# Two transformer blocks on one core: moving the rows of the first matmul operand inside its buffer

## The chip, the cores and the metric

The kernel runs on one core of one Trainium2 chip. The metric is the device time of one execution in microseconds; before the change it is 2463.79 us, the median of 3 runs (2463.78 to 2463.86).

## The reference, cut to what matters

Two blocks follow each other on 256 tokens of width 2048, everything in float32. The first has 16 meta tokens ahead of the 256.

```python
# first block: D = 2048, D_FF = 5632
z = rmsnorm(h) @ w_in                 # q, k, v, gate_b, gate_c, hc, forget logits
y = concat(forgetting_attention(q, k, v, log_f), gate_b * short_conv(gate_c * hc))
h = h + rmsnorm_by_group(y) @ w_out
h = h + (silu(n @ w_gate) * (n @ w_up)) @ w_down        # n = rmsnorm(h)
x = rmsnorm(h)[:, 16:]
# second block: D_FF_2 = 8192
q, k, v, u, gate_attn, gate_pool = split(x @ w_in_2)
merged = sigmoid(gate_attn) * (attention(q, k, v) @ w_ba) + sigmoid(gate_pool) * (pool(u) @ w_bp)
x = layer_norm(a * x + merged @ w_out_2)
x = layer_norm(a * x + square(relu(x @ w_ff1)) @ w_ff2)
```

Nearly all of the work is the products with the weights. Everything between them is small.

## The kernel before, in words

**A product in three parts.** Every float32 matrix is split into a high and a low part, each of a type (float32r) that TensorE takes at one column a cycle. A product A x W is computed as high A x high W, low A x high W and high A x low W. Here W is the stationary operand (128 x 128) and A, stored with features on the partitions and tokens along the free axis, is the moving one. An output tile of 128 features x 256 tokens is summed in a PSUM bank over all K tiles (pieces of 128 input features), and there are 16 of those for a width of 2048.

**Steps.** Weights stream from memory in units of 128 x 1024 float32 (512 KB) that hold two K tiles for a block of four output tiles. ScalarE copies a unit to `w_hi` (L842), VectorE subtracts to get `w_lo` (L1235), and four units are kept split. A step of TensorE's program is one unit for one output tile, in the code of `product_step`. For the 256 tokens it takes four matmuls, called a group below:

1. L606: `w_hi` of the even K tile times high and low rows at once, 512 columns (bank halves 0 and 1)
2. L607: `w_lo` of the even K tile times the high row, 256 columns
3. L609: `w_lo` of the odd K tile times its high row, 256 columns
4. L610: `w_hi` of the odd K tile times its high and low rows, 512 columns

Then the same two K tiles follow for the next of the four output tiles. Stages with 272 or 258 columns do not fit two rows in a bank and take three matmuls for each K tile (L613 to L615) instead.

**Two operands.** Stages alternate between operand buffers `a_op` and `b_op`, so that one can be filled while the other is read. `a_op` is used in two ways. Early, for the stages k, f, q, v and conv, K tile kt is at `a_op[:, kt, i, 0:272]`, with i 0 for high and 1 for low. Later the same memory is seen through `a_late`, which has 8 rows of 1088 words, one for each pair of K tiles, and is used for gu, k2, q2, v2, u, gate, out2 and ff2. `part` gives one row of 256 columns in it, and `parts` gives both rows of a K tile as one access pattern of 2 x 256. ScalarE writes the high rows (L961, L1028, L1033, L1098) and VectorE the low rows (L1456, L1611, L1687) through `part`.

**Places.** The word place is used from here on for the byte offset of a row within its tensor modulo 256. In `a_late` and `b_op` the rows of a pair of K tiles start at words 48, 306, 564 and 822 in the order high, low, high, low, which is at places 192, 200, 208 and 216. The 1088 words of a pair are 17 x 256 bytes, so that every pair has the same places. `h`, `a_op`, `b_op`, `raw`, `w_hi` and `w_lo` are allocated one after another with sizes that are multiples of 256 bytes, so places in them compare with each other. A 128-column slice of the weights starts at a multiple of 512 bytes, which is place 0. In the early use with 256 columns (stage q and the gate_b tiles of conv), the even K tile has its high row at place 64 and its low row at 128, and the odd K tile has them at 192 and 0.

**What sets the order.** The order of every engine is written out by a plan (`make_plan`) and semaphores, and no address enters it. TensorE's program goes on with the next unit when VectorE has split it (`lo_split`).

Of the kernel before, what the change touches and what calls it, by code (L numbers as in the profile page):

```python
# [19 lines left out]
TOK = META + SEQ  # L20
# [161 lines left out]
def two_blocks(nc, w, tokens, params, consts, mask1, mask2, positions, out):  # L182
# [5 lines left out]
    with ExitStack() as ctx:  # L188
        def sb(name, shape, dt=F32):
            return ctx.enter_context(nc.sbuf_tensor(name, shape, dt))  # L190
# [3 lines left out]


        ROW, PLACE = SEQ + 2, 48
        ROWS2 = 32 + HEADS
        h = sb("h", [P, KT, TOK])
        a_op = sb("a_op", [P, KT, 2, TOK], F32R)
        a_late = a_op[:, :, :, :].rearrange("p k i t -> p (k i t)").rearrange("p (m c) -> p m c", m=KT // 2)  # L200
        b_op = sb("b_op", [P, KT // 2, 4 * TOK], F32R)
# [21 lines left out]

        last_slot = b_op[0:ROWS2, KT // 2 - 1, PLACE + 2 * ROW:PLACE + 4 * ROW]
        cneg, pick = last_slot[:, 0:TOK], last_slot[:, TOK:TOK + HEADS]
# [9 lines left out]
        out_bank = [ctx.enter_context(nc.psum_tensor(f"out_bank{i}", [P, 512], F32)) for i in range(OUT_BANKS)]  # L235
        side_bank = [ctx.enter_context(nc.psum_tensor(f"side_bank{i}", [P, 512], F32)) for i in range(2)]

        def part(op, kt, i, n=SEQ):

            at = PLACE + ROW * (2 * (kt % 2) + i)  # L240
            return op[:, kt // 2, at:at + n]

        def parts(op, kt, n=SEQ):
            at = PLACE + ROW * 2 * (kt % 2)
            return op[:, kt // 2, at:at + 2 * ROW].rearrange("p (i t) -> p i t", i=2)[:, :, 0:n]

        def affine_column(i, x):
            rows = b_op[:, :, PLACE:PLACE + 4 * ROW].rearrange("p m (o i t) -> p m o i t", o=2, i=2)
# [137 lines left out]
        def tiles_at(step, part, *stages):  # L386

            for t in finish.get(step - max(0, part - 1), ()):
                if t.stage in stages and t.stage != "pool":
                    yield t  # L390
# [107 lines left out]
        def tensor_program(eng):  # L498
            t_ = Lane(eng)

            def take_side(kind, key, sem_free, value):

                i = len(side_release)
                if i >= 2:
                    t_.wait_ge(*side_release[i - 2])
                side_release.append((sem_free, value))
                side_of[kind, key] = side_bank[i % 2]
                return side_bank[i % 2]
# [28 lines left out]
            def moving(blk, cols, kt):  # L537

                if blk.operand == "a" and blk.stage not in ("k", "f", "q", "v", "conv"):
                    return part(a_late, kt, 0), part(a_late, kt, 1), parts(a_late, kt)  # L540
                if blk.operand == "a":
                    lo, hi = {"all": (0, TOK), "pair": (META, TOK), "conv": (META - 2, TOK)}[cols]
                    return a_op[:, kt, 0, lo:hi], a_op[:, kt, 1, lo:hi], a_op[:, kt, :, lo:hi]
                n = ROW if cols == "affine" else SEQ
                return part(b_op, kt, 0, n), part(b_op, kt, 1, n), parts(b_op, kt, n)
# [113 lines left out]
            def first_mixer(step):  # L659
# [17 lines left out]
                if (hd := head_at(step, CONV0)) is not None:  # L677
                    bank = take_side("scores", hd, masked, 2 * hd + 2)
                    sel = pick[:, hd:hd + 1].to_broadcast([ROWS2, P])
                    t_.wait_ge(q_scaled, hd + 1)  # L680
# [543 lines left out]
        def vector_program(eng):  # L1224
# [74 lines left out]
            def first_mixer(step):  # L1299
# [6 lines left out]
                if step == FORGET:  # L1306
# [11 lines left out]
                    v_.e.tensor_scalar(z, z, bf, None, ALU.add).then_inc(forget_step)  # L1318
                    v_.e.tensor_scalar(cneg, row[0:ROWS2, :], 0.0, None, ALU.mult).then_inc(rows_zeroed)
                if step == FORGET + 15:  # L1320
# [10 lines left out]
                    v_.wait_ge(forget_step, 10)  # L1331
                    v_.e.scalar_tensor_tensor(cneg[32:ROWS2, :], csum, -1.0, cneg[H8, :].bitcast(F32), ALU.mult,
                                              ALU.subtract).then_inc(forget_step)
                    v_.wait_ge(consts_landed, 16)
                    v_.e.tensor_tensor(pick, ident[0:ROWS2, H8], ident[0:ROWS2, 32:ROWS2], ALU.add).then_inc(pick_ready)
                for tile in tiles_at(step, 1, "q"):
# [642 lines left out]
        block = ctx.enter_context(nc.Block())  # L1979
# [117 lines left out]
```

## Time and profile before

| | before |
|---|---|
| median of 3 runs | 2463.79 us |
| the profiled execution | 2463.61 us, its span 2461.8 us |
| granted TensorE clock, mean | 0.997 |
| PE busy | 2433.2 us (99%), 14730 matmuls |
| weight loads (PEld) busy | 2168.8 us (88%) |
| VectorE, ScalarE, GpSimd busy | 66%, 49%, 9% |
| DMA engines | 58% of their time in the weight queue, 182 GB/s from memory |

PE is TensorE's matmul side and PEld its weight-load side, which runs beside it. A matmul's end is modelled, so the duration of one is longer than its share of the engine: the next one starts before it. How often matmuls start tells what they cost.

### The profile page before, as it was taken

What the parts mean: (1) busy time and instruction counts of PE and PEld (TensorE: products, weight loads), DVE (VectorE), ACT (ScalarE), POOL (GpSimd) and SP (SyncE); (2) the same over time, 40 slices, a digit from 0 to 9 for tenths busy, and PEclk for the clock granted to TensorE, in tenths of its full rate; (3) what the DMA queues carried; (4) which work ended last, traced back from release to release, by engine and by line L of the source; (5) the groups of instructions that cost most, each with busy time, mean ns of one, the idle gap of its engine ahead of it and who ended that gap; (6) DMA issues with size and microseconds to landing.
All of it is one profiled execution on the core that took longest, in us unless ns stands there. A gap on an engine that the chain in (4) does not pass through costs nothing.

```text
span 2461.8 us, 36358 instructions
## 1 busy us (share of the span) xinstructions
PE 2433.2 (99%) x14730; PEld 2168.8 (88%) x14730; DVE 1623.4 (66%) x2474; ACT 1199.9 (49%) x1729; POOL 213.8 (9%) x231
## 2 busy tenths in 40 slices
PE   8999999999999999999999999999999999999996
PEld 8898998888888888888888888888998888888886
DVE  5646676766666665667677756678885665565667
ACT  6444545544444443545555654544554443443544
POOL 0001111000000000002221102033200000000022
PEclk9999999999999999999999999999999999999998
DMA  7554456665666566665555456665566666666663
GB/s 248 180 158 128 131 166 196 189 190 181 197 190 191 184 196 190 189 187 194 192 186 171 161 188 190 184 193 182 163 194 196 189 189 188 188 195 189 183 194 103
DMA packets 125752, 449.60 MB, mean 183 GB/s; under 512 B 13840, under 2 KB 16400, under 8 KB 125584
## 3 DMA queue, kind: packets, MB, share of 16 engines
q1 hardware_dynamic: 125296, 446.91, 58.2%
q8 instruction: 116, 1.90, 0.3%
q14 instruction: 52, 0.43, 0.0%
q10 hardware_dynamic: 288, 0.36, 0.0%
HBM read 445.12 MB, written 2.10 MB: 182 GB/s over the span
## 4 chain that ended last, share of the span: by engine, by line
PE 95%; DVE 3%; ACT 1%; issue 0%; DMA 0%; POOL 0%; ACTq 0%; POOLq 0%; DVEq 0%
PE out_bank L606 27%; PE out_bank L610 27%; PE out_bank L607 14%; PE out_bank L609 14%; PE out_bank L613 3%; PE out_bank L614 3%; PE out_bank L615 3%; DVE w_lo L1235 1%; ACT w_hi L842 0%; PE side_bank L725 0%; PE side_bank L716 0%; DVE h L1618 0%; DVE b_op L1680 0%; PE side_bank L740 0%; PE side_bank L686 0%
## 5 line engine op out<-in xcount | busy, mean ns | idle before, releaser
L1235 DVE TENSOR_TENSOR w_lo<-raw,w_hi 128x1024 fp32r<-128x1024 f32 x839 | 1040.4, 1243 | 594.8 <-ACT w_hi L842 590.7
L842 ACT CAST w_hi<-raw 128x1024 fp32r<-128x1024 f32 x840 | 877.9, 1049 | 958.0 <-PE out_bank L610 875.8
L606 PE MATMUL out_bank<-a_op,w_hi 128*128 128x512 f32 x1984 | 784.6, 395 | 1.2 <-DVE w_lo L1235 0.7
L610 PE MATMUL out_bank<-a_op,w_hi 128*128 128x512 f32 x1984 | 776.7, 391 | 0.0
L607 PE MATMUL out_bank<-a_op,w_lo 128*128 128x256 f32 x1984 | 558.9, 282 | 0.0
L609 PE MATMUL out_bank<-a_op,w_lo 128*128 128x256 f32 x1984 | 552.1, 278 | 0.0
L609 PEld LDWEIGHTS out_bank<-a_op,w_lo 128*128 128x128 f32 x1984 | 380.1, 192 | 84.4
L607 PEld LDWEIGHTS out_bank<-a_op,w_lo 128*128 128x128 f32 x1984 | 372.9, 188 | 76.9
L606 PE MATMUL out_bank<-b_op,w_hi 128*128 128x512 f32 x992 | 389.8, 393 | 0.0
L610 PE MATMUL out_bank<-b_op,w_hi 128*128 128x512 f32 x992 | 388.0, 391 | 0.0
L606 PEld LDWEIGHTS out_bank<-a_op,w_hi 128*128 128x128 f32 x1984 | 373.1, 188 | 3.3 <-DVE w_lo L1235 1.7
L610 PEld LDWEIGHTS out_bank<-a_op,w_hi 128*128 128x128 f32 x1984 | 373.0, 188 | 0.0
L607 PE MATMUL out_bank<-b_op,w_lo 128*128 128x256 f32 x992 | 279.7, 282 | 0.0
L609 PE MATMUL out_bank<-b_op,w_lo 128*128 128x256 f32 x992 | 275.8, 278 | 0.0
L609 PEld LDWEIGHTS out_bank<-b_op,w_lo 128*128 128x128 f32 x992 | 190.4, 192 | 42.0
L607 PEld LDWEIGHTS out_bank<-b_op,w_lo 128*128 128x128 f32 x992 | 186.3, 188 | 39.9
L606 PEld LDWEIGHTS out_bank<-b_op,w_hi 128*128 128x128 f32 x992 | 186.5, 188 | 0.0
L610 PEld LDWEIGHTS out_bank<-b_op,w_hi 128*128 128x128 f32 x992 | 186.5, 188 | 0.0
L1252 DVE TENSOR_TENSOR work<-work,out_bank 128x256 f32<-128x256 f32 x248 | 102.5, 416 | 118.2 <-ACT work L861 117.5
L613 PE MATMUL out_bank<-a_op,w_hi 128*128 128x258 f32 (+1 forms) x504 | 147.5, 293 | 0.0
L614 PE MATMUL out_bank<-a_op,w_hi 128*128 128x258 f32 (+1 forms) x504 | 144.1, 286 | 0.0
L615 PE MATMUL out_bank<-a_op,w_lo 128*128 128x258 f32 (+1 forms) x504 | 143.7, 285 | 0.0
(288 smaller groups left out, 1998.7 us busy)
## 6 DMA issues: line engine op xcount, KB each, us to landing
raw<-in_w_ff SPq DMA_DIRECT2D x256, 512.0 KB, 4.2
raw<-in_w_in SPq DMA_DIRECT2D x223, 512.0 KB, 3.8
raw<-in_w_gu SPq DMA_DIRECT2D x176, 512.0 KB, 4.2
raw<-in_w_down SPq DMA_DIRECT2D x88, 512.0 KB, 4.3
raw<-in_w_out SPq DMA_DIRECT2D x64, 512.0 KB, 4.1
raw<-in_w_ba SPq DMA_DIRECT2D x16, 512.0 KB, 4.3
raw<-in_w_bp SPq DMA_DIRECT2D x16, 512.0 KB, 4.2
out<-h SPq DMA_DIRECT2D x8, 256.0 KB, 2.1
```

What stands on the lines that cost most here:

```text
L606: t_.e.matmul(bank[:, :], wh, a_both, start=start, stop=False, skip_group_check=True)
L607: mm = t_.e.matmul(bank[:, 0:SEQ], wl, a_hi, start=False, stop=stop, skip_group_check=True)
L609: t_.e.matmul(bank[:, 0:SEQ], wl, a_hi, start=False, stop=False, skip_group_check=True)
L610: mm = t_.e.matmul(bank[:, :], wh, a_both, start=False, stop=stop, skip_group_check=True)
L613: t_.e.matmul(to, wh, a_hi, start=start, stop=False, skip_group_check=True)
L614: t_.e.matmul(to, wh, a_lo, start=False, stop=False, skip_group_check=True)
L615: mm = t_.e.matmul(to, wl, a_hi, start=False, stop=stop, skip_group_check=True)
L842: a.e.copy(w_hi[:, m % SPLIT, :], raw[:, u % RAW, :]).then_inc(hi_split)
L1235: v_.e.tensor_tensor(w_lo[:, m % SPLIT, :], raw[:, u % RAW, :], w_hi[:, m % SPLIT, :].bitcast(F32), ALU.subtract).then_inc(lo_split)
L1252: v_.e.tensor_tensor(y, y, bank_of(tile)[:, 0:SEQ], ALU.add).then_inc(bank_free)
```

## The change

Only the offsets of the rows in `a_late` change. `b_op` keeps its own, and the early use of `a_op` is not touched. The table `A_ROWS` has an entry for each four K tiles, and in it the high and low offsets in words of the even and of the odd K tile:

| K tiles | order in memory | places before: high, low; high, low | places now |
|---|---|---|---|
| 0 to 3 | high, high, low, low | 192, 200; 208, 216 | 192, 200; 192, 200 |
| 4 to 7 | high, high, low, low | 192, 200; 208, 216 | 208, 216; 208, 216 |
| 8 to 11 | high, high, low, low | 192, 200; 208, 216 | 64, 72; 64, 72 |
| 12 to 15 | high, low, high, low | 192, 200; 208, 216 | 184, 192; 200, 208 |

From a high row to its low row it is 514 words in the first three, and 258 words before and in the last. Modulo 1024 bytes both are 8 bytes. No instruction is added, removed or moved on any engine; the matmuls, the writes of the rows and all waits stay as they are, with other addresses.

```diff
+        A_ROWS = (((48, 562), (304, 818)), ((52, 566), (308, 822)), ((16, 530), (272, 786)), ((46, 304), (562, 820)))
...
+        def rows_at(op, kt):
+
+            block = 4 * TOK * (kt // 2)
+            if op is b_op:
+                return block + PLACE + ROW * 2 * (kt % 2), block + PLACE + ROW * (2 * (kt % 2) + 1)
+            hi, lo = A_ROWS[kt // 4][kt % 2]
+            return block + hi, block + lo
+
         def part(op, kt, i, n=SEQ):
 
-            at = PLACE + ROW * (2 * (kt % 2) + i)
-            return op[:, kt // 2, at:at + n]
+            at = rows_at(op, kt)[i]
+            return op[:, :, :].rearrange("p m c -> p (m c)")[:, at:at + n]
 
         def parts(op, kt, n=SEQ):
-            at = PLACE + ROW * 2 * (kt % 2)
-            return op[:, kt // 2, at:at + 2 * ROW].rearrange("p (i t) -> p i t", i=2)[:, :, 0:n]
+            hi, lo = rows_at(op, kt)
+            flat = op[:, :, :].rearrange("p m c -> p (m c)")
+            return flat[:, hi:hi + 2 * (lo - hi)].rearrange("p (i t) -> p i t", i=2)[:, :, 0:n]
```

## Rows read from the trace of the kernel before

**Rows 1.** The page: busy time, and the granted clock in 40 slices

```profile
PE 2433.2 (99%) x14730; PEld 2168.8 (88%) x14730; DVE 1623.4 (66%) x2474; ACT 1199.9 (49%) x1729; POOL 213.8 (9%) x231
...
PEclk9999999999999999999999999999999999999998
```

**Rows 2.** The page: chain of work that ended last, by engine

```profile
PE 95%; DVE 3%; ACT 1%; issue 0%; DMA 0%; POOL 0%; ACTq 0%; POOLq 0%; DVEq 0%
```

**Rows 3.** Waits of PE: who for whom, us in total, times, longest

```profile
PE out_bank L568 <- DVE a_op L1240: 6.9, 1, 6.9
PE side_bank L805 <- POOL acc L1961: 0.8, 1, 0.8
PE out_bank L606 <- DVE w_lo L1235: 0.7, 1, 0.7
```

**Rows 4.** Groups of instructions, whole span: busy us, mean ns, idle before

```profile
L1235 DVE TENSOR_TENSOR w_lo<-raw,w_hi 128x1024 fp32r<-128x1024 f32 x839 | 1040.4, 1243 | 594.8 <-ACT w_hi L842 590.7
L842 ACT CAST w_hi<-raw 128x1024 fp32r<-128x1024 f32 x840 | 877.9, 1049 | 958.0 <-PE out_bank L610 875.8 <-PE out_bank L615 77.7 <-DMA raw<-in_w_in 4.1
L606 PE MATMUL out_bank<-a_op,w_hi 128*128 128x512 f32 x1984 | 784.6, 395 | 1.2 <-DVE w_lo L1235 0.7 <-DVE h L1262 0.3
```

**Rows 5.** Timeline of PE in stage ff2: start us, duration us

```profile
2000.22 0.39 PE L606 MATMUL out_bank<-a_op,w_hi 128*128 128x512 f32 x1
2000.45 0.28 PE L607 MATMUL out_bank<-a_op,w_lo 128*128 128x256 f32 x1
2000.57 0.28 PE L609 MATMUL out_bank<-a_op,w_lo 128*128 128x256 f32 x1
2000.68 0.39 PE L610 MATMUL out_bank<-a_op,w_hi 128*128 128x512 f32 x1
...
2084.11 0.39 PE L606 MATMUL out_bank<-a_op,w_hi 128*128 128x512 f32 x1
```

**Rows 6.** Groups of PE and PEld, 1997 to 2085 us (stage ff2, `a_late`)

```profile
L606 PE MATMUL out_bank<-a_op,w_hi 128*128 128x512 f32 x128 | 50.2, 392 | 0.0
L610 PE MATMUL out_bank<-a_op,w_hi 128*128 128x512 f32 x127 | 49.7, 391 | 0.0
L607 PE MATMUL out_bank<-a_op,w_lo 128*128 128x256 f32 x127 | 35.8, 282 | 0.0
L609 PE MATMUL out_bank<-a_op,w_lo 128*128 128x256 f32 x127 | 35.3, 278 | 0.0
...
L609 PEld LDWEIGHTS out_bank<-a_op,w_lo 128*128 128x128 f32 x127 | 24.4, 192 | 5.4
L610 PEld LDWEIGHTS out_bank<-a_op,w_hi 128*128 128x128 f32 x127 | 23.9, 188 | 0.0
```

**Rows 7.** Groups of PE, 95 to 105 us (stage q, early places)

```profile
L610 PE MATMUL out_bank<-a_op,w_hi 128*128 128x512 f32 x15 | 6.0, 397 | 0.0
L606 PE MATMUL out_bank<-a_op,w_hi 128*128 128x512 f32 x15 | 5.8, 390 | 0.0
L607 PE MATMUL out_bank<-a_op,w_lo 128*128 128x256 f32 x15 | 4.1, 275 | 0.0
L609 PE MATMUL out_bank<-a_op,w_lo 128*128 128x256 f32 x14 | 3.9, 281 | 0.0
```

**Rows 8.** Timeline of PE in stage q, a first stretch and a second

```profile
80.61 0.40 PE L606 MATMUL out_bank<-a_op,w_hi 128*128 128x512 f32 x1
...
87.61 0.39 PE L606 MATMUL out_bank<-a_op,w_hi 128*128 128x512 f32 x1
...
94.97 0.39 PE L606 MATMUL out_bank<-a_op,w_hi 128*128 128x512 f32 x1
...
105.36 0.39 PE L606 MATMUL out_bank<-a_op,w_hi 128*128 128x512 f32 x1
```

**Rows 9.** Groups of PE, 1724 to 1818 us (stage ff1, `b_op`, 258 columns)

```profile
L614 PE MATMUL out_bank<-b_op,w_hi 128*128 128x258 f32 x251 | 71.7, 286 | 0.0
L613 PE MATMUL out_bank<-b_op,w_hi 128*128 128x258 f32 x251 | 71.1, 283 | 0.2 <-DVE w_lo L1235 0.2
L615 PE MATMUL out_bank<-b_op,w_lo 128*128 128x258 f32 x251 | 70.7, 282 | 0.0
```

**Rows 10.** Timeline of PE in stage v (272 columns): one unit of two K tiles

```profile
117.54 0.28 PE L613 MATMUL out_bank<-a_op,w_hi 128*128 128x272 f32 x1
...
118.29 0.28 PE L613 MATMUL out_bank<-a_op,w_hi 128*128 128x272 f32 x1
```

## The prediction, made before the kernel was run

> **What bounds the kernel now.** I read the page first: TensorE is busy 99% of the span at a full granted clock [rows 1]. The chain of waits gives 95% of the span to PE [rows 2], and its own waits come to 6.9 us at the start and some 2 us after that [rows 3]. So the time is the sum of the intervals at which matmuls start. VectorE idles 595 us before its splits, nearly all of it for ScalarE, and ScalarE idles 958 us before its own, 876 us of it for PE [rows 4]. Both could follow a faster PE.
>
> The view that decides is the timeline, because durations overlap. In stage ff2 a group of four matmuls starts 2000.22 us and another 2084.11 us, 121 groups later: 83.89 / 121 = 693.3 ns for a group [rows 5]. Its 1536 columns take 640 ns at 2.4 GHz, so 53 ns of each group is something else, and that is all a change of addresses can touch. The durations there are 392, 282, 278 and 391 ns for L606, L607, L609 and L610, sum 1343 [rows 6]. Less 693.3, they overlap by 649.7, or 162.4 ns each. So the intervals are 229.6, 119.6, 115.6 and 228.6 ns. L607 and L609 have the same width and differ by 4 ns. What differs is the place of the high row, 192 against 208, and the weight load beside the first takes 192 ns against 188 (it is the one issued under L609's name) [rows 6]. So something at the level of 4 ns does depend on where and when the two streams read.
>
> **How many groups are touched.** L606 on `a_op` runs 1984 times [rows 4]. Stage q has 8 tiles of 8 pairs of K tiles, the gate_b tiles of conv as many, and those 128 read the early layout. That leaves 1856 groups, 464 for each entry of the table. At 693.3 ns they are 1287 us, 52% of the span. One ns a group over one entry is 464 x 1 ns = 0.46 us; over all four, 1.86 us.
>
> **Parts that cost nothing.** No instruction is added, removed or moved, and no wait. ScalarE and VectorE write the rows at new offsets; even if each write cost more, both engines idle long before their units [rows 4], and PE's waits for them are under 1 us each after the start [rows 3]. If that cover were gone, the 112 pairs of writes (32 for the norms, 16 for out2, 64 for ff2) would each have to be late by 45 ns to make 5 us.
>
> **What each entry should cost.** Stage q reads other places, so it prices more of them. From 95 to 105 us the durations are 390, 275, 281 and 397 ns [rows 7], again 1343, hence 227.6 (high at 64, low at 128), 112.6 (high at 64), 118.6 (192) and 234.6 ns (192 with low at 0). I take the price of a matmul from the place of its high row:
>
> - K tiles 0 to 3 (192 and 192): L606 229.6, L607 119.6, L609 by the two rows at 192, 118.6 to 119.6, L610 229.6. Sum about 698, 4.6 ns over 693.3.
> - K tiles 4 to 7 (208 and 208): 228.6, 115.6, 115.6, 228.6. Sum 688.4, 4.9 under.
> - K tiles 8 to 11 (64 and 64): 227.6, 112.6, 112.6, 227.6. Sum 680.4, 12.9 under. No row has low at 72.
> - K tiles 12 to 15 (184 and 200, lows at 192 and 208): no row has these. The nearest have high at 192 and 208: 693.4, the same as now. In ff1, with 258 columns, the matmul that reads rows at 200 and 216 takes 286 ns and the two that read 192 and 208 take 283 and 282 [rows 9], so a high row 8 bytes off may cost up to 3.5 ns in L607 and L609 each. I take half, 3.5 for the group.
>
> Straight sum: 4.6 - 4.9 - 12.9 + 3.5 = -9.7 ns, times 464 = -4.5 us.
>
> A second reading says that a sum of single prices is not how it goes. Stage q and ff2 have different single intervals and still the same group, 693.3. A first stretch of q runs at (87.61 - 80.61) / 10 = 700.0 ns and a later one at 10.39 / 15 = 693, with the same addresses [rows 8]. In columns at 2.4 GHz these are 1680 and 1664, which is 105 and 104 times 16. A unit of stage v takes 0.75 us, near 113 times 16 [rows 10]. It looks as if a repeated group falls into steps of 16 columns (64 bytes of a row), 6.7 ns. One step over one entry is 6.67 x 464 = 3.1 us. Rounded to steps the four entries are 0 or +1, -1 or 0, -2 to 0, 0 or +1. I take one step off for K tiles 4 to 7, one for 8 to 11, and one step back in total for the other two: net -3.1 us. Bounds on an entry from the nearest rows: 2 x 227.6 + 2 x 112.6 = 680.4 from below, and 2 x 234.6 + 2 x 119.6 = 708.4 from above. For all four that is -24 us to +28 us.
>
> **Where a rule speaks against this.** L607 and L609 differ by 4 ns at the same width [rows 6]. The Trainium skill, TensorE: Matmul & The Clock Gate, in its step by step on a matmul, has the moving operand and the weight load on separate read ports that take nothing from each other, and under back-to-back issue gap it gives N/2.4 + 2.5 ns, which for 256 columns is 109 ns wherever they lie. By that rule the change is worth nothing, the first rival below; the trace is 6 to 10 ns over it and not equal for equal widths, so I trust it little for the size, more for the sign being open.
> The rows at 200 and 216 cost 3 to 4 ns more in ff1 [rows 9]. The Trainium skill, SBUF — State Buffer, section on specifications, gives 16-byte lines with a penalty at each crossing. Rows at 184 and 200 start in the middle of a line and touch 65 instead of 64. With the full 3.5 ns in each of L607 and L609 of the last entry the sum would be 1.6 us higher.
>
> **The rivals.**
>
> 1. Nothing changes: every entry falls into the 1664 columns into which both layouts of the trace fall [rows 5, 8]. Time 2463.8. For: two unlike layouts agree. Against: 700.0 exists too.
> 2. Slower: both small matmuls of a group now read the same place, and the contention with the weight load that the trace shows once in a group (192 ns beside L607) comes twice. Then the group takes at least 4 ns more, and rounded up one step: +3.1 us an entry, for all four +12.4 us, 2476. It decides when weight loads of L609 and L610 both take about 192 ns. For: the place 192 with 119.6 ns is now used twice in the first entry. Against: at 208 and at 64 loads and matmuls run without it, and the place of the last entry differs by 16 bytes as before. If it hits two entries it is +6 us, 2470.
> 3. A larger gain: all entries lose a step or more, as the single prices for 64 would allow. Four steps are -12.4 us, 2451.4; with two at 64, -15.5. For: 112.6 ns is seen in the trace. Against: in the same group L610 then took 6 ns more, so what one matmul gained another gave back [rows 7].
>
> **How the numbers follow.** The profiled execution took 2463.61 us with a span of 2461.8; the median is 0.2 us above it, and I take differences from 2463.8. Forecast 2463.8 - 3.1 = 2460.7, its own range 2457.6 (two net steps) to 2463.8 (none). Chances: forecast 0.40, rival 1 0.17, rival 2 0.26, rival 3 0.17. A measurement can tell about 0.2%, 4.9 us. Faster than 2458.9: rival 3 and over half of the forecast's range, 0.39. Within: the rest of it and rival 1, 0.35. Slower than 2468.7: rival 2, 0.26. The range that holds 8 in 10 goes to 2452 and to 2473; what lies outside is the end of rival 3 and the upper half of rival 2. The full bounds above are not used because they need the worst or best place in all four matmuls of all entries.
>
> **What would show it.** In the timeline of ff2, groups of K tiles 0 to 3, 4 to 7, 8 to 11 and 12 to 15 follow each other in units, four tiles each unit, so the period can be read for every entry apart: 693 or 700, 687, 687 or 680, 693 or 700 ns. `b_op` stages must stay at 693.3. If a period is not a step of 6.7 ns from 693.3, the second reading is wrong. If all four are 693.3, rival 1 holds. Weight loads of 192 ns next to L607 and L609 alike speak for rival 2. PE waits of more than a few us for `w_lo` or an operand would mean that something other than addresses moved, and the prediction would be wrong in kind.

## The result

The changed kernel takes 2488.07 us (median of 4 runs, 2487.65 to 2488.41), the kernel before 2463.78 us on the same chip (4 runs, 2463.45 to 2463.86): ratio 1.0099, interval 1.0086 to 1.0111, or 24.3 us slower. The forecast was 2460.7 us in a range of 2452 to 2473: wrong in sign and outside the range. The profiled execution took 2488.18 us with a span of 2486.4, 24.6 over the span before.

In the code of after every line below the table stands 11 further down: L606, L607, L609, L610 are L617, L618, L620, L621; L842 is L853; L1235 is L1246. First its page, which answers to [rows 1, 2]:

```profile
PE 2458.6 (99%) x14730; PEld 2180.4 (88%) x14730; DVE 1622.4 (65%) x2474; ACT 1199.7 (48%) x1729; POOL 213.7 (9%) x231
...
PEclk9999999999999999999999999999999999999998
...
PE 96%; DVE 3%; ACT 1%; issue 0%; DMA 0%; POOL 0%; ACTq 0%; POOLq 0%; DVEq 0%
```

PE's waits in after, in the columns of [rows 3]:

```profile
PE out_bank L579 <- DVE a_op L1251: 6.6, 1, 6.6
PE side_bank L816 <- POOL acc L1972: 0.8, 1, 0.8
PE out_bank L617 <- DVE w_lo L1246: 0.6, 1, 0.6
```

Same counts, same clock, same waits. PE's busy time grew by 25.4 us, which holds the whole difference. The groups of instructions of after, against [rows 4]:

```profile
L1246 DVE TENSOR_TENSOR w_lo<-raw,w_hi 128x1024 fp32r<-128x1024 f32 x839 | 1039.4, 1242 | 615.4 <-ACT w_hi L853 614.2
L853 ACT CAST w_hi<-raw 128x1024 fp32r<-128x1024 f32 x840 | 877.5, 1048 | 983.1 <-PE out_bank L621 900.4
L617 PE MATMUL out_bank<-a_op,w_hi 128*128 128x512 f32 x1984 | 792.4, 399 | 0.6 <-DVE w_lo L1246 0.6
...
L617 PE MATMUL out_bank<-b_op,w_hi 128*128 128x512 f32 x992 | 389.9, 393 | 0.0
```

ScalarE's idle time behind PE grew from 876 to 900 us: it waits for a slower PE and takes no longer itself. The matmul of L617 on `a_op` went from 395 to 399 ns; the same instruction on `b_op` stayed at 393.

Where in `a_op`: the timeline of one tile block in stage ff2 of after (start us, duration us). From row to row lie 8 groups, which is one entry of the table (2 pairs of K tiles, 4 tiles each). The last two rows are the start of the `b_op` stage behind it and of the stage after that, 128 groups apart.

```profile
2015.84 0.39 PE L617 MATMUL out_bank<-a_op,w_hi 128*128 128x512 f32 x1
...
2021.49 0.40 PE L617 MATMUL out_bank<-a_op,w_hi 128*128 128x512 f32 x1
...
2027.15 0.40 PE L617 MATMUL out_bank<-a_op,w_hi 128*128 128x512 f32 x1
...
2032.82 0.40 PE L617 MATMUL out_bank<-a_op,w_hi 128*128 128x512 f32 x1
...
2038.49 0.39 PE L617 MATMUL out_bank<-a_op,w_hi 128*128 128x512 f32 x1
...
2106.43 0.39 PE L617 MATMUL out_bank<-b_op,w_hi 128*128 128x512 f32 x1
...
2195.21 0.39 PE L617 MATMUL out_bank<-a_op,w_hi 128*128 128x512 f32 x1
```

The steps are 5.65, 5.66, 5.67 and 5.67 us; divided by 8, and with the third decimal of the trace, 706.2 ns a group for K tiles 0 to 3, 707.9 for 4 to 7, 708.4 for 8 to 11, 708.1 for 12 to 15. Before it was 693.3 [rows 5]. All four entries are slower by 13 to 15 ns, two steps of 6.7 ns, and not one is faster. `b_op` takes 88.78 us for 128 groups, 693.6 with the switch in it.

Summed by stage, the late first operand costs 24.0 us more, 12.9 ns over its 1856 groups: for instance +1.84 us in one ff2 stage of 128 groups, +2.76 us in each of three gu stages of 192. The stretch before stage q adds 0.6 us, although its addresses are those of before. The other early stages and the `b_op` stages are within 0.04 us each.

The single matmuls of the first two entries, K tiles 0 to 3 and then 4 to 7, in after (columns of [rows 6]); loads stand under the name of the matmul they load for:

```profile
L617 PE MATMUL out_bank<-a_op,w_hi 128*128 128x512 f32 x8 | 3.2, 396 | 0.0
L621 PE MATMUL out_bank<-a_op,w_hi 128*128 128x512 f32 x8 | 3.2, 394 | 0.0
L620 PE MATMUL out_bank<-a_op,w_lo 128*128 128x256 f32 x8 | 2.3, 285 | 0.0
L618 PE MATMUL out_bank<-a_op,w_lo 128*128 128x256 f32 x8 | 2.3, 282 | 0.0
...
L620 PEld LDWEIGHTS out_bank<-a_op,w_lo 128*128 128x128 f32 x8 | 1.5, 192 | 0.3
L618 PEld LDWEIGHTS out_bank<-a_op,w_lo 128*128 128x128 f32 x8 | 1.5, 192 | 0.3
```

```profile
L621 PE MATMUL out_bank<-a_op,w_hi 128*128 128x512 f32 x9 | 3.5, 393 | 0.0
L617 PE MATMUL out_bank<-a_op,w_hi 128*128 128x512 f32 x8 | 3.2, 400 | 0.0
L618 PE MATMUL out_bank<-a_op,w_lo 128*128 128x256 f32 x8 | 2.3, 284 | 0.0
L620 PE MATMUL out_bank<-a_op,w_lo 128*128 128x256 f32 x8 | 2.2, 280 | 0.0
...
L618 PEld LDWEIGHTS out_bank<-a_op,w_lo 128*128 128x128 f32 x8 | 1.5, 189 | 0.3
```

In the first entry two loads take 192 ns, as rival 2 had it. In the second none takes over 189 ns, and its groups are as slow (707.9 against 706.2 ns). So the long load is not what sets the period. Taken apart as in the prediction (sum of durations less the period, in four parts), the second entry's intervals are 237.7, 121.7, 117.7 and 230.7 ns, where the prediction had 228.6, 115.6, 115.6, 228.6.

### The profile page after: what moved, and what is told of

Its sections match the earlier page's. It is cut to its first block, busy times and chain, and to the rows that moved or that the text cites. A ratio compares the mean times of both kernels' runs of the same rounds, so it can differ in the third digit from the quotient of the medians.

```text
span 2486.4 us, 36358 instructions
## 1 busy us (share of the span) xinstructions
PE 2458.6 (99%) x14730; PEld 2180.4 (88%) x14730; DVE 1622.4 (65%) x2474; ACT 1199.7 (48%) x1729; POOL 213.7 (9%) x231
## 4 chain that ended last, share of the span: by engine, by line
PE 96%; DVE 3%; ACT 1%; issue 0%; DMA 0%; POOL 0%; ACTq 0%; POOLq 0%; DVEq 0%
PE out_bank L617 28%; PE out_bank L621 27%; PE out_bank L618 14%; PE out_bank L620 14%; PE out_bank L624 3%; PE out_bank L625 3%; PE out_bank L626 3%; DVE w_lo L1246 1%; PE side_bank L736 0%; ACT w_hi L853 0%; PE side_bank L727 0%; PE side_bank L751 0%; PE side_bank L697 0%; PE side_bank L720 0%; DMA h<-in_tokens 0%
## 5 line engine op out<-in xcount | busy, mean ns | idle before, releaser
L1246 DVE TENSOR_TENSOR w_lo<-raw,w_hi 128x1024 fp32r<-128x1024 f32 x839 | 1039.4, 1242 | 615.4 <-ACT w_hi L853 614.2
L853 ACT CAST w_hi<-raw 128x1024 fp32r<-128x1024 f32 x840 | 877.5, 1048 | 983.1 <-PE out_bank L621 900.4
L617 PE MATMUL out_bank<-a_op,w_hi 128*128 128x512 f32 x1984 | 792.4, 399 | 0.6 <-DVE w_lo L1246 0.6
L621 PE MATMUL out_bank<-a_op,w_hi 128*128 128x512 f32 x1984 | 785.3, 396 | 0.0
L620 PE MATMUL out_bank<-a_op,w_lo 128*128 128x256 f32 x1984 | 558.8, 282 | 0.0
L618 PE MATMUL out_bank<-a_op,w_lo 128*128 128x256 f32 x1984 | 558.8, 282 | 0.0
L620 PEld LDWEIGHTS out_bank<-a_op,w_lo 128*128 128x128 f32 x1984 | 375.7, 189 | 89.1
L618 PEld LDWEIGHTS out_bank<-a_op,w_lo 128*128 128x128 f32 x1984 | 376.8, 190 | 86.0
L617 PE MATMUL out_bank<-b_op,w_hi 128*128 128x512 f32 x992 | 389.9, 393 | 0.0
L621 PE MATMUL out_bank<-b_op,w_hi 128*128 128x512 f32 x992 | 388.1, 391 | 0.0
L621 PEld LDWEIGHTS out_bank<-a_op,w_hi 128*128 128x128 f32 x1984 | 375.1, 189 | 0.0
L617 PEld LDWEIGHTS out_bank<-a_op,w_hi 128*128 128x128 f32 x1984 | 372.8, 188 | 2.3 <-DVE w_lo L1246 1.1
L618 PE MATMUL out_bank<-b_op,w_lo 128*128 128x256 f32 x992 | 279.7, 282 | 0.0
L620 PE MATMUL out_bank<-b_op,w_lo 128*128 128x256 f32 x992 | 275.9, 278 | 0.0
L620 PEld LDWEIGHTS out_bank<-b_op,w_lo 128*128 128x128 f32 x992 | 190.3, 192 | 42.1
L618 PEld LDWEIGHTS out_bank<-b_op,w_lo 128*128 128x128 f32 x992 | 186.3, 188 | 40.1
L621 PEld LDWEIGHTS out_bank<-b_op,w_hi 128*128 128x128 f32 x992 | 186.5, 188 | 0.0
L617 PEld LDWEIGHTS out_bank<-b_op,w_hi 128*128 128x128 f32 x992 | 186.5, 188 | 0.0
L624 PE MATMUL out_bank<-a_op,w_hi 128*128 128x258 f32 (+1 forms) x504 | 147.5, 293 | 0.0
```

The costliest lines, as they stand in the source:

```text
L617: t_.e.matmul(bank[:, :], wh, a_both, start=start, stop=False, skip_group_check=True)
L618: mm = t_.e.matmul(bank[:, 0:SEQ], wl, a_hi, start=False, stop=stop, skip_group_check=True)
L620: t_.e.matmul(bank[:, 0:SEQ], wl, a_hi, start=False, stop=False, skip_group_check=True)
L621: mm = t_.e.matmul(bank[:, :], wh, a_both, start=False, stop=stop, skip_group_check=True)
L624: t_.e.matmul(to, wh, a_hi, start=start, stop=False, skip_group_check=True)
L853: a.e.copy(w_hi[:, m % SPLIT, :], raw[:, u % RAW, :]).then_inc(hi_split)
```

## The experiments

Five kernels (e1, e4, e5, e6, e10) run the four matmuls of a group alone, over operands of zeros, and leave out the rest of the reference. A layout there is the words (4 bytes) at which high row 0, low row 0, high row 1 and low row 1 start in a pair's block: before is 48, 306, 564, 822. Periods are means over whole stretches of a layout. The seven others are whole kernels, written as diffs against the changed one. All edits are shown shortened, with `...` or in words for what is left out. The first matmul of a group, L617 in the changed kernel, is L115 in e1, L67 in e6, L66 in e10, L618 in e11 and L624 in e12.

**e1: do the addresses alone give the periods?**

```
+for hi0, lo0, hi1, lo1, w in LAYOUTS:            # 51 layouts, 64 groups of each
+    ...
+            matmul(to, w_hi[w + at0], both(hi0, lo0)); matmul(to[0:SEQ], w_lo[w + at0], row(hi0))
+            matmul(to[0:SEQ], w_lo[w + at1], row(hi1)); matmul(to, w_hi[w + at1], both(hi1, lo1))
+    matmul(bank0[0:128], w_hi[0:P], a_op[0:128])      # parts one layout from the next
```

> A kernel of TensorE's groups alone: the four matmuls of a group on zeros, with the four output tiles and eight pairs of K tiles of the real program, 64 groups for each of 51 layouts of the rows, and no other engine at work (it computes nothing of the reference and stores the tokens). Theory 1, places: the period of a group is set by where its rows lie against the weights, by TensorE's two streams alone. Then the layout of before has 693 ns here too, the four new ones 704 to 712 as in the trace of the changed kernel, and before's places with lows 1024 bytes further away (memory order high, high, low, low) stay at 693. Theory 2, distance: a 2 x 256 pattern whose halves are 2056 bytes apart instead of 1032 reads slower. Then before's places with far lows go up by 10 ns or more and the new places with near lows come down to 693. Theory 3, writers: the rows collide with what ScalarE and VectorE write. Then all 51 are alike at about 693. The shifts of all four rows by 8 bytes to 192 bytes tell whether the whole matters against the weights or only the rows against each other: by theory 1 moving the weights by as much the other way gives the same periods.

The timeline of this kernel, first with the places of after's K tiles 0 to 3, rows 56 groups apart, then with the places of before twice, each 56 groups: as they were, and in the order high, high, low, low at equal places modulo 256, with the low rows 3080 and 4104 bytes behind their high rows instead of 1032.

```profile
66.01 0.40 PE L115 MATMUL out_bank<-a_op,w_hi 128*128 128x512 f32 x1
...
105.59 0.40 PE L115 MATMUL out_bank<-a_op,w_hi 128*128 128x512 f32 x1
...
247.33 0.39 PE L115 MATMUL out_bank<-a_op,w_hi 128*128 128x512 f32 x1
...
286.16 0.39 PE L115 MATMUL out_bank<-a_op,w_hi 128*128 128x512 f32 x1
291.87 0.39 PE L115 MATMUL out_bank<-a_op,w_hi 128*128 128x512 f32 x1
...
330.70 0.39 PE L115 MATMUL out_bank<-a_op,w_hi 128*128 128x512 f32 x1
```

39.58 / 56 = 706.8 ns, and 38.83 / 56 = 693.4 for both others. The four entries of the change gave 706.7, 706.7, 710.0 and 703.3. The same places in the old order (high, low, high, low) gave about 706.7, 706.7 and 710. So the places modulo 256 carry it, and neither the order in memory nor the distance from high to low does, nor anything that writes the rows. All four rows moved by a common amount: 8 bytes 700, 16 bytes 706.7, 32 bytes 710, 128 bytes either way 693.4, -8 bytes 703.3, -32 bytes 693.3. The weights alone moved, rows as they were: 8 bytes 706.6, 16 bytes 699.9, 32 bytes 693.3, 64 bytes 709.9, 128 bytes 693.4. All 51 lie between 693.3 and 713.3. No layout was below before's.

**e2: the four entries on other quarters of the K tiles, the last quarter as before.**

```
-A_ROWS = (((48, 562), (304, 818)), ((52, 566), (308, 822)), ((16, 530), (272, 786)), ((46, 304), (562, 820)))
+A_ROWS = (((16, 530), (272, 786)), ((48, 562), (304, 818)), ((52, 566), (308, 822)), ((48, 306), (564, 822)))
```

> The real program with the layouts given to other K tiles: places 64 to K tiles 0 to 3, 192 to 4 to 7, 208 to 8 to 11, and K tiles 12 to 15 as before. Theories 1 and 2: the periods go with the layout, 704 to 712 ns in the first twelve K tiles and 693.3 in the last four, so that about a quarter of the 24.3 us comes back: 2481 to 2483. If instead some K tiles are slow whatever their layout, the last four stay at 708 and the time at 2488.

2481.47 us, ratio 1.0072 (1.0055 to 1.0089), 17.8 over before. In ff2 the quarter with before's rows was back at 693.4 ns (two pairs, 8 groups in 5.55 us), the others at 706.5 to 710 wherever they stood. The period goes with the layout and not with the K tile. Against after, 6.6 us came back: that is the last entry's share. The first pair with before's rows, right behind another layout, is already at 693.3 (2027.42 to 2030.20 us, 4 groups): this switch cost nothing.

**e3: only the 8-byte move of the last K tiles.**

```
+A_ROWS = (((48, 306), (564, 822)), ((48, 306), (564, 822)), ((48, 306), (564, 822)), ((46, 304), (562, 820)))
```

> The real program of before with the 8-byte move of K tiles 12 to 15 alone: places 184, 192, 200, 208, distance and order as before. Theory 1: the quarter keeps its 13 to 16 ns a group, 464 x 14 = 6.5 us, 2470.3. Theory 2 (distance or order) gives nothing for this quarter: 2463.8.

2471.57 us, ratio 1.0032 (1.0020 to 1.0044), +7.9. The timeline of one tile block in ff2 of this kernel, starts of pairs 0, 1, 2, 6, 7 and of pair 0 of the next block; a pair is 4 groups:

```profile
2025.57 0.39 PE L617 MATMUL out_bank<-a_op,w_hi 128*128 128x512 f32 x1
...
2028.38 0.39 PE L617 MATMUL out_bank<-a_op,w_hi 128*128 128x512 f32 x1
...
2031.15 0.39 PE L617 MATMUL out_bank<-a_op,w_hi 128*128 128x512 f32 x1
...
2042.24 0.40 PE L617 MATMUL out_bank<-a_op,w_hi 128*128 128x512 f32 x1
...
2045.07 0.39 PE L617 MATMUL out_bank<-a_op,w_hi 128*128 128x512 f32 x1
...
2047.90 0.39 PE L617 MATMUL out_bank<-a_op,w_hi 128*128 128x512 f32 x1
```

Pairs 6 and 7 take 2.83 us, 707 ns a group; pairs 2 to 5 take 11.09 / 16 = 693. Pair 0 has its old places and yet takes 2.81 / 4 = 702: this switch back from another layout costs once some 34 ns (4 x 8.5). With 58 such blocks (1856 / 32) that makes 2.0 us, against the 1.4 us measured over the 6.5 expected. Summed by stage, 7.4 of the 7.9 us are in the late first operand and 0.7 us in the stretch before stage q, which this edit does not touch.

**e4: 100 layouts, to find the rule.**

```
+LAYOUTS = [before, three with rows and weights moved together, D, ...] + 95 drawn at random   # 32 groups each
```

> The groups alone again, 32 for each of 100 layouts: before, three in which rows and weights are moved together by 8, 32 and 64 bytes, the 8-byte move of the last K tiles, and 95 drawn at random among those that fit in the 1088 words of a pair, in six orders of memory. Theory 1, only the rows' places against the weights' count: the three common moves have before's 693.3 ns. The alternative, that places count against something fixed in the memory, gives them other periods, as it does when rows alone move. The random ones say how special 693.3 is: the first map had 17 shifts of the four rows together between 693.3 and 710 with a mean near 703; I expect a mean of 702 to 706, all in steps of 3.3 ns, under one in ten at 693.3, and perhaps one or two a step lower. If many are under 693.3, the prediction's rival 3 was a matter of picking better places.

Rows and weights moved together by 32 or 64 bytes: 693.3 as before. Together by 8 bytes: 713.0. So it is not only the distance between the two streams. That they do count against each other is plain at 64 bytes: rows alone moved gave 700.0 (e1), weights alone 709.9 (e1), both together 693.3. Most of the 95 random ones lie on steps of 3.3 ns from 693.3 to 720, the most frequent within 0.3 ns of 700.0 (25) and of 706.7 (21), the mean about 704. What is a multiple of 16 columns is the time after which the pattern repeats, which can be one, two or three groups: 703.3 is the mean of 697 and 709 ns in turn (e1), and the few means between the steps, such as 708.9, fit three groups in turn. 9 of the 95 have 693.3, none less. Before's layout was among the best; a random move away from it costs 11 ns in the mean.

**e5: are other engines' reads and writes part of it?**

```
+        def scalar_program(e):  for i in range(400): e.copy(to_act[:, i % 2, :], raw[:, 0, :])
+        vector_program:         for i in range(340): e.tensor_tensor(to_dve[:, i % 2, :], raw[:, 0, :], raw[:, 1, :], subtract)
```

> The groups alone with ScalarE copying and VectorE subtracting 128x1024 float32 in the memory all the while, for ten of the layouts. Theory 1 (TensorE's two read streams among themselves): all periods as without traffic, 693.3 for before, 707, 707, 710 and 703.5 for the four new ones. If other engines' reads and writes take part, the periods rise or lose their steps, and the 8-byte move goes from 703.5 towards the 708 to 709 that it has in the real program.

Both engines are at work up to 394 us of the span of 467, over eight of the ten layouts and part of the ninth: before 693.3, the changed entries 706.6, 706.6, 709.8 and 703.5, and stage q's layout, the ninth, 699.8. Nothing moved by more than 0.2 ns from e1. DMA writes were no part of it. One exception is a finding: rows moved by 32 bytes gave 710.0 in e1 and 693.3 here. One layout can have two periods.

**e6: what comes ahead of a layout.** The whole sequence of 8 pairs as in the kernel, and single layouts entered after one matmul of 128 to 156 columns.

```
-for hi0, lo0, hi1, lo1, w in LAYOUTS:
+for pairs, w, passes, columns in SEGMENTS:
+    ... for m, (hi0, lo0, hi1, lo1) in enumerate(pairs):
-    matmul(bank0[0:128], w_hi[0:P], a_op[0:128])
+    matmul(bank0[0:columns], w_hi[0:P], a_op[0:columns])
```

> The groups alone, now to test what a group inherits from the one before it. Segment 2 has the layouts of the changed kernel pair by pair, segment 3 those of the kernel with the 8-byte move alone, without anything between; then rows and weights moved together by 8, 16, 24 and 32 bytes; then three layouts, each entered eight times after a matmul of 128 to 156 columns. Theory 1a, places and the entered phase: segment 3 shows the moved pairs at 706 to 709 as in the real program, not 703.5, and the first pair after them at about 702 although its own places are those of before; the shifted layout, 710 in one run and 693.3 in another, shows both here, by the width of the matmul ahead of it. Theory 1b, places alone: moved pairs 703.5, the first pair 693.3, and each layout one period at all eight widths. Common moves: if lines of 16 bytes count, 16 and 32 bytes give 693.3 and 8 and 24 bytes 700 or more.

The changed kernel's eight pairs alone: 707.5 (706.0 without the pass that begins after the added matmul), 706.7, 709.2, 706.7, 706.9, 710.0, 709.6, 706.7 ns, as in the program. Before's rows with e3's last two pairs: 702.5, five times 693.3, 708.1, 706.7: e3 again, with no other engine running. Rows and weights together by 8, 16, 24, 32 bytes: 713.0, 706.6, 700.0, 693.5. The branch that had 16 bytes neutral fell: of these moves only 32 bytes is. Timeline of one layout (before's rows moved by 32 bytes), each time 26 groups, entered first from before's layout after a matmul of 156 columns, then from itself after one of 128 (in the code the matmul stands behind its stretch, so it sets the entry of the next):

```profile
694.40 0.40 PE L67 MATMUL out_bank<-a_op,w_hi 128*128 128x512 f32 x1
...
712.86 0.40 PE L67 MATMUL out_bank<-a_op,w_hi 128*128 128x512 f32 x1
...
717.21 0.40 PE L67 MATMUL out_bank<-a_op,w_hi 128*128 128x512 f32 x1
...
735.49 0.40 PE L67 MATMUL out_bank<-a_op,w_hi 128*128 128x512 f32 x1
```

18.46 / 26 = 710.0 and 18.28 / 26 = 703.1 (two groups in turn, mean 703.3): same addresses, another phase of entry, and it stays for the whole stretch. Phase is a word for what the matmuls ahead leave behind; the runs show its effect and not what it is. Before's own layout has 693.3 at all eight widths. The 8-byte move has 706.7 at all eight, where e1, e4 and e5 had 703.3: it too has two periods. The 693.3 that e5 had for the layout of the timeline did not come up here.

**e7: the order high, high, low, low by itself, at places that e4 has at 693.3.**

```
+A_ROWS = (((6, 556), (286, 814)), ((6, 556), (286, 814)), ((6, 556), (286, 814)), ((48, 306), (564, 822)))
```

> The real program with the memory order high, high, low, low in K tiles 0 to 11, at a set of places that had 693.3 ns alone: words 6, 286, 556, 814, that is high rows at 24 and 120 and low rows at 176 and 232, from high to low 2200 and 2112 bytes; K tiles 12 to 15 as before. Theory 1: the order costs nothing and the time is that of before, 2463 to 2465. Theory 2, order or distance: three quarters of the 24.3 us, 2482.

(The second low row is at place 184; the 232 above is a slip.) 2469.43 us (11 runs), ratio 1.0023 (1.0014 to 1.0032), +5.7: the expectation of 2463 to 2465 missed. The timeline of one block in ff2, starts of pairs 0, 1, 6, 7 and of the next block:

```profile
2023.37 0.40 PE L617 MATMUL out_bank<-a_op,w_hi 128*128 128x512 f32 x1
...
2026.17 0.39 PE L617 MATMUL out_bank<-a_op,w_hi 128*128 128x512 f32 x1
...
2040.04 0.40 PE L617 MATMUL out_bank<-a_op,w_hi 128*128 128x512 f32 x1
...
2042.89 0.40 PE L617 MATMUL out_bank<-a_op,w_hi 128*128 128x512 f32 x1
...
2045.66 0.40 PE L617 MATMUL out_bank<-a_op,w_hi 128*128 128x512 f32 x1
```

Pairs 1 to 5 take 13.87 / 20 = 693 ns: the order costs nothing. Pair 0 takes 700 and pair 6 takes 712, the first pairs after a switch of layout. Two good layouts beside each other cost 2.80 + 2.85 - 8 x 0.6933 = 0.10 us a block, 6.0 us over 58 blocks, where 5.7 were measured.

**e8: the 8-byte move in all K tiles.**

```
+A_ROWS = (((46, 304), (562, 820)),) * 4
```

> The real program with the 8-byte move in all K tiles: one layout throughout (words 46, 304, 562, 820), so that no group is entered from another layout. If part of the 24.3 us comes from mixing layouts, this tells it from the places: alone this layout has 703.3 or 706.7 ns, by how it is entered, and keeps what it starts with, so (10.0 to 13.3) x 1856 = 18.6 to 24.8 us, 2482.4 to 2488.6, with the same period in all pairs and none at 708 to 710. If the period were set by places alone, 703.3 throughout and 2482.4.

2485.64 us, ratio 1.0090 (1.0076 to 1.0104), +22.2. The ff2 stages run at 706.7 ns but for the first, which is at 703.3 in every pair: the two periods that the groups alone had, in the real program. Most stages lose 13.3 ns a group; k2 to gate, out2 and the first ff2 stage lose 8 to 10, hence less than the full 24.7 us (13.3 x 1856). This kernel keeps the order of before and has nine tenths of the change's loss.

**e9: another layout with 693.3 ns, in the late first operand.** Its rows 16, 276, 544, 806 come from e4, where it had the same period as before's layout. It is called the tied layout below.

```
+A_ROWS = (((16, 276), (544, 806)),) * 4
```

> The real program with another layout that had 693.3 ns alone, in all K tiles: words 16, 276, 544, 806 in the order high, low, high, low, all four places different from before's (high rows at 64 and 128, low rows at 80 and 152). If the period decides and 693.3 is a floor, the time is that of before, 2462.8 to 2464.8: no layout among 150 was lower, so none is expected to beat it. If the real program's other parts (entering from b_op, the products of the attention between) favour before's places, it is 1 to 4 us slower.

2461.66 us (11 runs), ratio 0.9993 (0.9984 to 1.0002): not told from before, though below the expected 2462.8. The floor that the expectation was built on did not hold: in unbroken runs after a disturbance, groups take 686.7 ns, a step below anything seen until here. In the last ff2 stage these two rows are 81 groups apart:

```profile
2379.87 0.39 PE L617 MATMUL out_bank<-a_op,w_hi 128*128 128x512 f32 x1
...
2435.49 0.39 PE L617 MATMUL out_bank<-a_op,w_hi 128*128 128x512 f32 x1
```

55.62 / 81 = 686.7. Before's layout has 693.3 in the same stretch, so the two layouts share one period and not the other.

**e10: which entry puts that layout into the lower step?** One matmul of 16 to 256 columns ahead of it, in steps of 8.

```
+SEGMENTS = [(before's pairs, c), (tied pairs, c), ... for c in range(16, 257, 8)]
```

> The groups alone. In the run with the tied layout (16, 276, 544, 806) in all of the late operand, a part of the groups runs at 686.7 ns, a step below the 693.3 that no layout of the map went under: they come in unbroken runs that begin after a disturbance. Here 32 groups of that layout follow 8 groups of before's layout, or 8 of their own, and one matmul of 16 to 256 columns in steps of 8. If a group inherits its phase, some widths give 686.7 for all 32 groups and others 693.3, by the width alone. If 686.7 needs the other engines' work, none does.

After before's layout the lower step came at 64, 80, 112 and 200 columns, after the layout itself only at 248. The timeline at 104 columns and at 112, 28 groups each:

```profile
378.61 0.39 PE L66 MATMUL out_bank<-a_op,w_hi 128*128 128x512 f32 x1
...
398.02 0.39 PE L66 MATMUL out_bank<-a_op,w_hi 128*128 128x512 f32 x1
...
406.60 0.39 PE L66 MATMUL out_bank<-a_op,w_hi 128*128 128x512 f32 x1
...
425.82 0.39 PE L66 MATMUL out_bank<-a_op,w_hi 128*128 128x512 f32 x1
```

19.41 / 28 = 693.2 and 19.22 / 28 = 686.4; with the third decimal of the trace, 693.4 and 686.7. Eight columns are 3 ns once, and 6.7 ns in every group after them.

**e11: the tied layout in both operands, so that no switch lies between stages.**

```
+A_ROWS = (((16, 276), (544, 806)),) * 4
-            if op is b_op:
-                return block + PLACE + ROW * 2 * (kt % 2), block + PLACE + ROW * (2 * (kt % 2) + 1)
```

> The real program with the tied layout in both operands and in all K tiles, so that no stage is entered from another layout. A state once entered should last from stage to stage until other products of TensorE disturb it. If it stays in the share of the run before (about one group in seven at 686.7 ns in the late first operand), the time is 1 to 3 us below before's, 2461 to 2463. If the low state is entered early in the long undisturbed stages (gu, down, ff1, ff2), most of the 2848 groups gain 6.7 ns: down to 2446. If 693.3 is entered instead, or the 258-column products of the second operand lose, 2463 to 2466.

(A helper that reads one column of `b_op` follows the new places.) 2458.42 us (7 runs, 2453.71 to 2459.44), ratio 0.9971 (0.9960 to 0.9983), -5.3, between the branches of the expectation. In the profiled execution 626 groups run at 686.7 and some 2150 at 693.3. Three runs fall near 2454 and four near 2459. As the program is the same in all, the lower step presumably holds longer in some than in others; only one of the four was profiled.

**e12: and one matmul of 248 columns ahead of the first `down` and the first ff2 group of tiles.**

```
+                        if start and x == 0 and u == kicked.get((blk.stage, blk.group)):
+                            t_.e.matmul(bank[:, 0:248], w_hi[:, slot, 0:P], kick_row, start=True, stop=True, ...)
```

> The tied layout in both operands, with one more matmul of 248 columns (about 0.1 us each) ahead of the first group of two stages, down of group 0 (near 520 us) and ff2 of group 0 (near 1815 us); its product is overwritten and goes into nothing. In the groups alone, 248 columns after groups of the same layout at 693.3 took the next 32 to 686.7, and no other width of 16 to 256 in steps of 8 did. In the run without them the stages from 520 to 1163 us and from 1815 to 2350 us are at 693.3 throughout, some 927 and 770 groups. If the entered phase decides in the real program too and lasts until other products come between, these go to 686.7: 11 us less, 2446 to 2449. If only the first of the two or its stage holds, 2452 to 2457. If the phase at those two places is not that of the test, nothing but the two matmuls is added: 2458 to 2460.

2453.13 us (5 runs, 2452.81 to 2454.69), ratio 0.9958 (0.9944 to 0.9971), 10.4 us faster than before and 35 faster than the change, in the branch where only the first of the two matmuls acts. The timeline of e12 around the added matmul, and 914 groups on; then of e11, 906 groups of the same stages:

```profile
521.76 0.28 PE L619 MATMUL out_bank<-a_op,w_hi 128*128 128x248 f32 x1
...
523.25 0.39 PE L624 MATMUL out_bank<-b_op,w_hi 128*128 128x512 f32 x1
...
1150.87 0.39 PE L624 MATMUL out_bank<-b_op,w_hi 128*128 128x512 f32 x1
```

```profile
521.68 0.39 PE L618 MATMUL out_bank<-b_op,w_hi 128*128 128x512 f32 x1
...
1149.84 0.39 PE L618 MATMUL out_bank<-b_op,w_hi 128*128 128x512 f32 x1
```

627.62 / 914 = 686.7 against 628.16 / 906 = 693.3. In these two executions a matmul that computes nothing of use, and costs some 0.1 us, gains 6 us. The times of whole runs say it less plainly: all five of e12 are at 2455 or less, but so are three of e11's seven, without the matmul. The second one, at 1810.79 us behind matmuls of 258 columns, did nothing. In all 1426 groups ran at 686.7.

## Why the prediction was wrong

**What bounds the kernel, how many groups, parts that cost nothing.** Right. PE at full clock, 1856 groups, no new wait, the writers hidden: 24.0 of the 24.3 us are in the periods of those groups, and `b_op` stayed. The four entries' periods alone (e1) give 464 x (13.4 + 13.4 + 16.7 + 10.0) ns = 24.8 us.

**The step that failed: "I take the price of a matmul from the place of its high row".** The periods predicted from it were 698, 688.4, 680.4 and 697 ns, measured 706.2, 707.9, 708.4 and 708.1. The price of one row does not exist apart from the others. High at 208 with low at 216 took 228.6 ns in L610 of before; in the second entry L617 reads rows at the same two places and takes 237.7. What differs is the rest of the group. High at 64 had 112.6 ns in stage q; the two in K tiles 8 to 11 take 120 and 117. In e1 the weights alone, moved by 8 bytes, change the period by two steps with every row where it was. What has a period is the whole layout: four rows and the weights together, and the phase in which it is entered.

**The last entry** was taken at 3.5 ns a group, 1.6 us for 464 groups. e2 has it at 6.6 us and e3 at 7.9: over four times as much, and part of it is the switch (e3).

**The second reading: steps of 6.7 ns.** Right in form: before, the changed entries, e1, e4 and e10 give 686.7, 693.3, 700.0, 706.7, and where a mean lies between, two or three kinds of group take turns. But I took its sign from the failed sum. The trace had nothing below 693.3, in either of its two layouts, and a 700.0 above it [rows 8]; that is little evidence, but what there was pointed the other way. e4 shows how things stood: 9 of 95 random layouts are as good as before's and none is better, so a change of layout without a rule nearly always loses.

**Rival 1 (nothing changes)** was refuted in all four entries. **Rival 2 (slower)** had the sign. Its mechanism, a 192 ns load twice in a group, is present in the first entry and absent in the second, at equal periods; its time, 2476, has one step an entry where two were measured. **Rival 3** fell.

**The range.** The bound that I worked out, +28 us, held the result (24.3). I left it out because it needed the worst place in all four matmuls of all entries. The reason fails because the four intervals are not drawn one by one: the group as a whole sits on a step. A random layout costs 11 ns in the mean (e4), which over 1856 groups is 20 us, so the result is near what four layouts picked blindly would cost. The chances had a slip too: of the forecast's own range, 2457.6 to 2463.8, a fifth lies below 2458.9 and not over half, so that "faster" should have had about 0.25 and not 0.39. Either way most of the weight was on the wrong side.

**The two rules.** e1 moves only the weights, and the period goes from 693.3 to 706.6 ns; and a move by 64 bytes costs when rows or weights make it alone, and nothing when both do (e1, e4). The Trainium skill, TensorE: Matmul & The Clock Gate, step by step on a matmul, has the two reads on ports that take nothing from each other. By that no place would matter against another; for these matmuls the measurements decide against it, though they do not say where the two meet. In e6 rows and weights moved by 16 bytes cost 13 ns a group, by 32 bytes nothing. The Trainium skill, SBUF — State Buffer, section on specifications, gives lines of 16 bytes with a penalty at each crossing. A move of everything by 16 bytes changes no crossing and would be free by that alone; the measurement decides against it.

**Which cause is shown, and what is open.** Shown: the loss is in the place of the four rows modulo 256 together with the weights' place (e1, e2, e4, e8), without any part of other engines (e1, e5, e6), of the order high, high, low, low (e1, e7) or of the distance of high from low (e1). A switch of layout can cost by itself, 0.03 to 0.1 us (e3, e6, e7), and need not (e2). That both high rows are alike modulo 256, as in three of the entries, is not needed for the loss: e8 has them at 184 and 200 and loses nine tenths as much. Open: what in the hardware gives the steps of 16 columns and the two phases, what makes e11's runs fall into two kinds, and why the second added matmul of e12 did not act. No rule that gives the 151 periods of e1 and e4 from the addresses was found.

## What to carry to other kernels

When TensorE is the bound at full clock and its durations overlap, measure the period of the whole repeated group for each layout of operands, in a small kernel of the groups alone. e6, with the program's own sequence of layouts, reproduced its periods to about 1 ns; e1, with one layout at a time, was up to 5 ns off (703.3 against 708.1 for the last entry), as the layouts ahead count too. Don't build the period from the price of single matmuls, and keep one layout through neighbouring stages, since a switch can cost as well. Before moving operands of a kernel, ask where its layout stands among random ones: from the best one in ten, nearly every blind move loses.

## What the hardware showed that was not expected

- Four matmuls of 1536 columns in all take 686.7 to 720 ns by the operands' places and the entry, with mean about 704 over random places (e4, e10); 640 would be the columns at 2.4 GHz.
- The time after which the pattern repeats, one to three groups, is on a grid of 16 columns (6.7 ns), and a layout can have two or three periods: 693.3, 703.3 and 710.0 for one (e1, e5, e6), 703.3 and 706.7 for another (e1, e6, e8), 686.7 and 693.3 for a third (e10). The one it falls into can hold over hundreds of groups: 914 in e12, through changes of stage, with one layout in both operands.
- A common move of rows and weights by 32 bytes is neutral, by 8, 16 or 24 bytes costs 20, 13 and 7 ns (e6).
- One matmul of 248 columns ahead of 914 groups went with 686.7 instead of 693.3 ns in all of them (e12 against e11, one profiled execution each). The medians differ by 5.3 us, with e11's runs in two kinds, and 2453.13 us is the best median of this study.
